# SSD mixer: squares of the gated pairs moved from GpSimd to ScalarE, their group sums to VectorE

## The reference

```python
y = ssd_chunked_scan(xs * dt[..., None], dt * a, bm, cm)
y = y + xs * d_skip[:, None]
y = y.reshape(b, l, D_INNER) * jax.nn.silu(z)
y = rms_norm(y.reshape(b, l, SSD_GROUPS, D_INNER // SSD_GROUPS),
             norm_g.reshape(SSD_GROUPS, D_INNER // SSD_GROUPS))
```

## Time and profile before

| | us |
|---|---|
| median of 3 runs | 1722.72 (1719.02 to 1722.85) |
| profiled execution, its own time | 1722.89 |
| its span in the trace | 1721.1 |
| VectorE busy over the span | 1116.0 (65%) |
| GpSimd busy over the span | 113.4 (7%) |

### The profile page before, as it was taken

The page is one execution under the profiler, slowest core; times in us unless marked ns, Lnnn a source line. Parts: engine busy times, 40 slices in busy tenths (PEclk is TensorE's granted clock), DMA queues, the critical chain, the costliest instruction groups (busy, mean ns, idle before and its releaser), DMA issues.

```text
span 1721.1 us, 19811 instructions
## 1 busy us (share of the span) xinstructions
PE 1661.6 (97%) x7719; PEld 1317.0 (77%) x7719; DVE 1116.0 (65%) x1417; ACT 736.8 (43%) x1026; POOL 113.4 (7%) x118
## 2 busy tenths in 40 slices
PE   5999998999999999999999999998999999999998
PEld 2888776888888887887666778875668888888887
DVE  3788867532455567877999955546758886652364
ACT  3443322221222236557887424537842364431241
POOL 0005100000000000000233100002410000000000
PEclk9999998999999999999999999998999999999999
DMA  9444322222222232222121222220012222222222
GB/s 387 160 193 183 134 74 73 98 98 98 98 98 98 98 126 93 75 98 74 50 74 50 77 95 84 104 73 26 1 75 97 98 98 98 98 98 98 98 98 98
DMA packets 25421, 174.16 MB, mean 101 GB/s; under 512 B 2800, under 2 KB 3184, under 8 KB 5104
## 3 DMA queue, kind: packets, MB, share of 16 engines
q1 hardware_dynamic: 21440, 146.52, 23.7%
q10 hardware_dynamic: 3888, 26.38, 3.9%
HBM read 168.69 MB, written 4.19 MB: 100 GB/s over the span
## 4 chain that ended last, share of the span: by engine, by line
PE 75%; DVE 16%; ACT 6%; issue 2%; DMA 2%; ACTq 0%; DVEq 0%
PE bank L1528 23%; PE bank L1529 23%; PE bank L1530 23%; DVE p L1263 3%; DVE w_lo L851 3%; ACT p L379 2%; DMA ada_chunk<-ada 2%; ACT pt L379 1%; PE bank L2045 1%; DVE clipped L1239 1%; PE bank L1727 1%; DVE rs_g L1292 1%; PE bank L1709 1%; DVE zt L1294 1%; DVE xbc L1231 1%
## 5 line engine op out<-in xcount | busy, mean ns | idle before, releaser
L1528 PE MATMUL bank<-h,w_hi 128*128 128x512 f32 x1200 | 475.8, 397 | 10.0 <-DVE w_lo L851 4.5
L1529 PE MATMUL bank<-h,w_hi 128*128 128x512 f32 x1200 | 470.0, 392 | 0.0
L1530 PE MATMUL bank<-h,w_lo 128*128 128x512 f32 x1200 | 470.0, 392 | 0.0
L379 ACT ACTIVATE w_hi<-raw 128x2048 fp32r<-128x2048 f32 (+1 forms) x129 | 246.6, 1911 | 335.1 <-DMA raw<-slabs 324.0
L851 DVE TENSOR_TENSOR w_lo<-raw,w_hi 128x2048 fp32r<-128x2048 f32 (+1 forms) x129 | 296.6, 2299 | 95.1 <-ACT w_hi L379 91.2
L1528 PEld LDWEIGHTS bank<-h,w_hi 128*128 128x128 f32 x1200 | 227.1, 189 | 62.1 <-issue 8.3
L1529 PEld LDWEIGHTS bank<-h,w_hi 128*128 128x128 f32 x1200 | 227.2, 189 | 47.9 <-issue 1.4
L1530 PEld LDWEIGHTS bank<-h,w_lo 128*128 128x128 f32 x1200 | 226.9, 189 | 48.0
L1528 PE MATMUL bank<-a_hi,w_hi 128*128 128x512 f32 x432 | 168.2, 389 | 1.7 <-DVE a_lo L857 1.7
L1529 PE MATMUL bank<-a_lo,w_hi 128*128 128x512 f32 x432 | 168.1, 389 | 0.0
L1530 PE MATMUL bank<-a_hi,w_lo 128*128 128x512 f32 x432 | 168.0, 389 | 0.0
(11 more groups left out here) (338 smaller groups left out, 2352.5 us busy)
## 6 DMA issues: line engine op xcount, KB each, us to landing
raw<-slabs SPq DMA_DIRECT2D x127, 1024.0 KB, 4.8
ada_chunk<-ada ACTq DMA_DIRECT2D x24, 1024.0 KB, 7.2
x<-x_in SPq DMA_DIRECT2D x4, 1024.0 KB, 8.5
spill_x<-x SPq DMA_DIRECT2D x1, 2048.0 KB, 11.7
x<-spill_x SPq DMA_DIRECT2D x2, 1024.0 KB, 6.1
out<-x SPq DMA_DIRECT2D x8, 256.0 KB, 2.0
raw<-slabs SPq DMA_DIRECT2D x2, 768.0 KB, 4.1
inv<-inv ACTq DMA_DIRECT2D x1, 1024.0 KB, 6.8
```

The costliest lines, as they stand in the source:

```text
L379: return act.activation(out, in_, f, **kw)
L1528: pe.matmul(out, w[0], a[0], start=start, stop=False)
L1529: pe.matmul(out, w[0], a[1], start=False, stop=False)
L1530: return pe.matmul(out, w[1], a[0], start=False, stop=stop)
```

## The change

The squares go to ScalarE as `Square` activations (`pair_square`), one turn behind: in turn `pair` the square of pair-1 stands between the exponentials of heads 2·pair+2 and 2·pair+3, and waits for `z_used`, pair. The sums go to VectorE (`add_square`): in turn `pair` the sum for pair-1 stands ahead of `weighted_scores(2·pair+3)`, and waits for the square. The last pair's square and sum stand behind the loop. GpSimd's loop goes; after it GpSimd works again only in the attention. Pairs 1 to 3 of a group share one buffer for their square, so the squares of pairs 2 and 3 of a group also wait for the sum before them.

```diff
@@ ScalarE
             for pair in range(XS_T):
                 half_tanh(pair)
                 if pair + 1 < XS_T:
-                    for hd in (2 * pair + 2, 2 * pair + 3):
-                        exponentials(hd)
+                    exponentials(2 * pair + 2)
+                if pair:
+                    pair_square(pair - 1)
+                if pair + 1 < XS_T:
+                    exponentials(2 * pair + 3)
                 if pair % 2:
                     weight_head(SLAB0["z"] + pair // 2 + 2)
+            pair_square(XS_T - 1)
...
+            def pair_square(pair):
+                act.wait_ge(sem("z_used"), pair + 1)
+                if pair % 4 >= 2:
+                    act.wait_ge(sem("square_added"), pair - pair // 4 - 1)
+                do.tell(fn(group_square(pair), xbc[:, pair, :], ACT.Square), "pair_squared", pair + 1)
@@ VectorE
+            def add_square(pair):
+                if pair % 4:
+                    dve.wait_ge(sem("pair_squared"), pair + 1)
+                    total = group_total(pair // 4)
+                    do.tell(dve.tensor_tensor(total, total, group_square(pair), ALU.add), "square_added", pair - pair // 4)
...
                     weighted_scores(2 * pair + 2)
                     if pair + 2 < XS_T:
                         diag_clipped(2 * pair + 4)
+                if pair:
+                    add_square(pair - 1)
+                if pair + 1 < XS_T:
                     weighted_scores(2 * pair + 3)
             gated_pair(XS_T - 1)
+            add_square(XS_T - 1)
             weight_tail(SLAB0["gates"] + 1)
@@ GpSimd
-            for pair in range(XS_T):
-                pool.wait_ge(sem("z_used"), pair + 1)
-                do(pool.tensor_tensor(group_square(pair), xbc[:, pair, :], xbc[:, pair, :], ALU.mult))
-                if pair % 4:
-                    total = group_total(pair // 4)
-                    do.tell(pool.tensor_tensor(total, total, group_square(pair), ALU.add), "square_added", pair - pair // 4)
```

## The result

The changed kernel takes 1725.88 us (median of 19 runs, 1722.89 to 1727.09) against 1722.54 for the kernel before (19 runs beside them, 1719.02 to 1724.90): a ratio of 1.0017 with a 95% interval of 1.0010 to 1.0023. It is 3.3 us slower. The interval excludes 1, so the loss is there, and it is less than the 0.3% which the prediction called no change.

The account below looks back on a forecast made before the run. VectorE was taken to bound turns 2 to 14 and behind the loop. Terms + 0.66, - 3.24, + 0.15, + 2.16, + 2.37, - 0.29 and + 1.50 summed to + 3.3 us: 1726.0 against the median, range 1720.5 to 1729.5.

Parts of the forecast that it names:

- Turn 1, + 0.66: In turn 1 the chain still comes from ScalarE, and one square in it adds 0.66 us.
- The give-back, 1.26 in each even turn: Even turns 2 to 12: without GpSimd, VectorE's `w_lo` gives back 0.29 and its product 0.97 us.
- The stops, 1.08: Turns 5, 9, 13: VectorE waits 1.08 us each for exponentials behind a square that waits for the gated pair.
- The three waits of 0.05: Turns 2, 6, 10: VectorE's second product waits 0.05 us for ScalarE, + 0.15 in all.
- Behind the loop, + 1.50: Ahead of the `weight_tail`, VectorE waits for the last square, then adds for 0.72: + 1.50 us.
- Turn 14: Only `w_lo`'s give-back of 0.29 us lies on the path; the products behind it run while TensorE works.
- The rival in which it becomes the bound: If TensorE's running sums wait twice the walk's 1.8 us per four turns, it falls behind: 1728.2 us; chance 0.10.
- The first rival: The stops in turns 5, 9, 13 don't come: - 0.1 us, 1722.7 us; chance 0.15.
- About 9.8 us of VectorE's stage is GpSimd in its way: Over the stage, GpSimd lengthens 32 products by 7.9 us and eight `w_lo` by 1.9 us.
- the 8.7 us on the path: VectorE's give-back from GpSimd's going: 6 x 1.26 in even turns, 3 x 0.29 in turns 5, 9, 13, 0.29 in turn 14.
- the price: 15 squares on VectorE: + 10.8 us, less ScalarE waits of 4.9; ScalarE held 6 us better.
- its roots end before VectorE's `w_lo`: Behind the loop, ScalarE's roots (1.28 table, 0.7) end before VectorE's `w_lo` (2.3), so the reciprocal doesn't move further.

Follow-up runs that it names:

- The first experiment: Changed kernel with the square behind the second head's exponentials in turns 5, 9 and 13 alone: 1722.34 us, ratio 1.0000 to the kernel before.
- The second experiment: Changed kernel with the last pair's add moved behind the `weight_tail`: 1725.66 us, ratio 1.0020 to the kernel before, stage 158.5 us.
- the two versions that gain: "the parts together", at 1721.16 us, and "The further step", at 1719.20 us.
- the parts together: Changed kernel with late squares in turns 1, 5, 9, 13, adds of pairs 2, 6, 10 on GpSimd, last add behind `weight_tail`: 1721.16 us, ratio 0.9992.
- The further step: "the parts together" with turn 2's square late, its add behind the second product, and the last add on GpSimd: 1719.20 us, ratio 0.9989.

## Why the prediction was right

The forecast was 1726.0 and the median is 1725.88; the sum was + 3.3 us and the stage has + 3.3. That the two times agree within 0.1 us is luck: the interval of the ratio leaves the shift anything from 1.7 to 4.0 us. That the stage agrees is not, since its parts do as well:

| stretch | before | after | shift | forecast |
|---|---|---|---|---|
| first clip to the `w_lo` of turn 2 | 29.19 | 29.85 | + 0.66 | + 0.66 |
| from there to the `w_lo` of turn 14 | 112.07 | 113.50 | + 1.43 | + 1.44 |
| from there to the first reciprocal | 14.67 | 15.88 | + 1.21 | + 1.21 |

Point by point:

- **Turn 1, + 0.66.** The product starts 25.37 us behind the first clip instead of 24.71, and ScalarE's chain releases it with one square of 0.63 in it. Its wait grew by more, from 0.19 to 1.13, because VectorE comes to it earlier: the product ahead of it takes 1.49, without GpSimd's square beside it.
- **The give-back, 1.26 in each even turn.** The products stand at 1492 ns and `w_lo` at 2291. I took the measured 0.97 per product and not the overlap of 1.10. The term and the adds of 0.72 come out together: four turns grew by 0.46 (37.37 to 37.83), and the terms give - 2.81 + 2.16 + 1.13 = + 0.48. With 1.10 they would give + 0.22.
- **The stops, 1.08.** Measured 1.12, 1.11 and 1.11. The first experiment removes just these three, and 3.1 us of the stage go with them; so the walk through the turn had the cause as well as the size. The three waits of 0.05 in turns 2, 6 and 10 don't show.
- **Behind the loop, + 1.50.** The wait is 0.81, and the add 0.72 with its gap. The second experiment covers the wait, and 0.8 us leave this part of the stage.
- **Turn 14.** I had not foreseen ScalarE's 0.75 there. It lies beside TensorE's work and cost nothing.
- **TensorE.** The rival in which it becomes the bound did not come; inside the loop nothing of VectorE's waits for it. Its running sums wait 0.50 us in turn 5 and 1.12 in turn 6, where I had 0.6 and 1.2. TensorE's timeline:

```profile
854.18 0.49 PE L1865 MATMUL bank<-acum_parts,pick 128*128 128x512 f32 x1 [0.50 <-ACT p L379]
...
863.95 0.50 PE L1865 MATMUL bank<-acum_parts,pick 128*128 128x512 f32 x1 [1.12 <-ACT p L379]
```

The first rival, that the stops don't come, is what the first experiment builds: it gave a ratio of 1.0000, where the rival's - 0.1 us is that too.

Three of its statements were less good. "About 9.8 us of VectorE's stage is GpSimd in its way" is a true reading of the rows, but it is no sum that one can win: of the 8.7 us on the path only 4.1 are to be had, since TensorE stands behind VectorE (its four turns take 36.0 by the prediction's own count, 1.4 less than VectorE's 37.37). For a change that loses, this didn't matter; the two versions that gain ran into it. And the squares on VectorE would cost 5.1, not 6: the price took 15 squares at 0.72 on VectorE's path and the waits that would go with ScalarE's. Two of the 15, those of pairs 13 and 14, fill waits of turn 14 and of the last pair and cost nothing, 1.4 us too much in the price. The expectation of that run left them out and was 0.6 too low. Against the changed kernel its trace has - 0.27 up to the `w_lo` of turn 2 (expected - 0.66: one square stands in turn 1 too), + 5.48 from there to turn 14 (expected + 5.25), and - 0.08 behind it.

The third is about ScalarE, and held only by what stands around it: that its roots end before VectorE's `w_lo` and don't move the reciprocal. With the last add off VectorE, in two of the experiments, the reciprocal waited 0.49 us for the root.

In the theories of the two versions that gain the same fault stands: I summed what VectorE's list loses, named TensorE only in the rivals, and did not follow ScalarE's list (turn 2 in the first version, the root in the second).

## What to carry to other kernels

Work that is moved to an engine with room on average must still be placed in that engine's list: ask what the new instruction waits for, and what stands behind it that doesn't need to wait. Here ScalarE had half a microsecond of room per turn (9.34 less 8.8), and three squares placed one step too early cost 3 us. And before a disturbance (here GpSimd's 8.7 us) is counted as a gain, look how far behind the next engine stands: leaving the whole work out is one run, and gives the ceiling.

## What the runs showed of the hardware

I had not expected TensorE's clock to differ between two executions of one kernel. Busy time by stretch of "the parts together" (us, then PE, PEld, DVE, ACT, POOL, granted clock, DMA share, GB/s):

```profile
810.00:815.00 5.00, 5.00 (x24) 3.58 (x24) 4.83 (x6) 4.67 (x11) 0.00 (x0) 1.00 0.00 0
...
995.00:1000.00 5.00, 3.50 (x11) 2.81 (x12) 4.79 (x7) 1.79 (x1) 0.00 (x0) 0.78 0.62 210
1000.00:1005.00 5.00, 5.00 (x21) 4.07 (x20) 2.69 (x2) 0.69 (x1) 0.00 (x0) 0.88 0.00 0
```

and of the same kernel again:

```profile
810.00:815.00 5.00, 4.22 (x12) 3.38 (x13) 3.85 (x5) 4.67 (x11) 0.00 (x0) 0.69 0.00 0
```

The second execution has 12 matmuls in that stretch for 24, at a clock of 0.69. A part of this is that its stage began 2.7 us later; but the run with the last add behind the `weight_tail`, whose stage began within 0.2 us of it, has 19 there at a clock of 1.00. At 995 to 1005 the granted clock is 0.78 and 0.88: with 1.2 GHz for 44% of one stretch and 24% of the next, that is 3.4 us at half clock, by estimate some 1.7 us of TensorE's work. TensorE had stood before both drops: 2.4 us for a `w_lo` in the first execution, 2.8 us for ScalarE's exponentials ahead of 810 in the second. But the changed kernel stands 2.4 us for its `w_lo` as well and has no drop there:

```profile
1000.00:1005.00 5.00, 2.56 (x12) 2.03 (x12) 4.83 (x6) 2.60 (x2) 0.00 (x0) 1.00 0.58 210
```

Of the ten traces six have a drop near 1000, and four (the kernel before and the changed one among them) have none; near 810 four have one. From the first reciprocal to the end the six with a drop near 1000 took 771.7 to 773.5 us (773.4 the first of these two executions), the four without 770.7 to 771.7. Inside the stage the two traces of "the parts together" differ by 0.6, and all of it lies in the last wait for TensorE, 2.10 us with the drop near 810 and 1.45 without. The further step has that drop as well and waits 2.03, so a part of what its stage missed may be this drop's. That the drops cause these differences fits the order of events and was not tried by itself. The larger spread lies elsewhere: in the ten traces the first clip comes 790.4 to 795.0 us after the start, in a part of the program that is the same in all; this was not followed. What decides whether a wait of that length brings a drop was not tried either, and stays open.
